# Order of tiles in the last attention, and smaller steps in a gated attention

## The reference

```python
def gla_mixer(h, w_in, w_gk2, b_gk, g_onorm, w_out):      # gated attention, 4 heads
    ...
    gk = gk_low @ w_gk2 + b_gk
    log_a = jax.nn.log_sigmoid(gk) / GLA_GATE_TAU
    b = jnp.cumsum(log_a, axis=3)                         # the gate sums, within chunks of 64
    q_e = q * jnp.exp(b); k_e = k * jnp.exp(-b)
    ...
    o = rms_norm(o, g_onorm).reshape(B, S, GLA_V)
    return (o * jax.nn.silu(gate)) @ w_out

def mla_mixer(h, positions, w_in, g_qa, w_qb, g_kva, w_kvb, w_out):   # last attention, 16 heads
    ...
    q = rms_norm(c_q, g_qa) @ w_qb                        # per head 128 plain + 64 rotary columns
    kv = rms_norm(c_kv, g_kva) @ w_kvb                    # per head 128 key + 128 value columns
    q = concatenate([q_nope, rope(q_rope)]); k = concatenate([k_nope, rope(k_rope)])
    p = softmax(causal(q @ k.T * scale))
    return (p @ v * silu(gate)) @ w_out
```

## Time and profile before

| | us |
|---|---|
| median of 3 runs | 2226.57 |
| lowest, highest | 2223.46, 2227.17 |
| the profiled execution | 2226.45 |
| its span | 2224.7 |
| TensorE busy in it | 2145.7 |
| VectorE busy | 1312.7 |
| ScalarE busy | 1158.4 |

### The profile page before, as it was taken

How to read it: one execution, slowest core, us unless ns; L and a number is a source line. 1 busy time by engine, 2 the same in 40 slices (tenths; PEclk the granted TensorE clock), 3 DMA queues, 4 the chain that set the end, 5 groups by cost and what they waited for, 6 DMA issues and landing times.

```text
span 2224.7 us, 46503 instructions
## 1 busy us (share of the span) xinstructions
PE 2145.7 (96%) x17596; PEld 2104.9 (95%) x17596; DVE 1312.7 (59%) x1641; ACT 1158.4 (52%) x1544; POOL 283.3 (13%) x325
## 2 busy tenths in 40 slices
PE   5999999999999999999999999999999979999996
PEld 5999999999999999999999999999998969899996
DVE  5655664544557666666765545655665465755644
ACT  5444545555546555555554444644554445656542
POOL 2000000010110111111111100001010123111112
PEclk8999999999999999999999999999999989999998
DMA  4454545555555555555545555445444434444453
GB/s 150 172 183 174 189 163 198 194 187 202 189 189 192 186 188 189 187 183 181 187 186 208 193 218 212 146 178 190 171 169 170 171 131 147 157 151 152 155 183 113
DMA packets 54927, 393.83 MB, mean 177 GB/s; under 512 B 6097, under 2 KB 6225, under 8 KB 7522
## 3 DMA queue, kind: packets, MB, share of 16 engines
q1 hardware_dynamic: 54432, 392.19, 49.2%
q10 hardware_dynamic: 450, 1.02, 0.1%
HBM read 391.09 MB, written 2.10 MB: 177 GB/s over the span
## 4 chain that ended last, share of the span: by engine, by line
PE 80%; issue 13%; POOL 3%; DVE 2%; ACT 2%; DMA 0%; POOLq 0%; DVEq 0%; ACTq 0%
PE acc L554 23%; PE acc L555 23%; PE acc L556 23%; PE tok L596 2%; PE tok L598 2%; PE tok L597 2%; POOL n_lo L1927 1%; POOL sumsq_g L1918 1%; PE att L614 1%; POOL x L1940 0%; POOL probs L2080 0%; DVE rstd L1345 0%; POOL probs L2077 0%; PE att L788 0%; PE att L864 0%
## 5 line engine op out<-in xcount | busy, mean ns | idle before, releaser
L1337 DVE TENSOR_TENSOR w_lo<-raw,w_hi 128x1024 fp32r<-128x1024 f32 x740 | 907.0, 1239 | 728.2 <-ACT w_hi L921 726.1
L921 ACT ACTIVATE w_hi<-raw 128x1024 fp32r<-128x1024 f32 x740 | 770.0, 1056 | 594.7 <-PE acc L556 363.5
L554 PE MATMUL acc<-n_hi,w_hi 128*128 128x256 f32 x3488 | 986.7, 283 | 26.8 <-POOL n_lo L1927 19.4
L555 PE MATMUL acc<-n_lo,w_hi 128*128 128x256 f32 x3488 | 979.6, 281 | 0.0
L556 PE MATMUL acc<-n_hi,w_lo 128*128 128x256 f32 x3488 | 979.4, 281 | 0.0
L554 PEld LDWEIGHTS acc<-n_hi,w_hi 128*128 128x128 f32 x3488 | 668.7, 192 | 30.1 <-issue 20.2
L555 PEld LDWEIGHTS acc<-n_lo,w_hi 128*128 128x128 f32 x3488 | 662.0, 190 | 0.5
L556 PEld LDWEIGHTS acc<-n_hi,w_lo 128*128 128x128 f32 x3488 | 660.8, 189 | 0.0
L555 PE MATMUL acc<-f_lo,w_hi 128*128 128x256 f32 x688 | 193.5, 281 | 0.0
L556 PE MATMUL acc<-f_hi,w_lo 128*128 128x256 f32 x688 | 193.5, 281 | 0.0
L554 PE MATMUL acc<-f_hi,w_hi 128*128 128x256 f32 x688 | 193.5, 281 | 0.0
(11 more groups left out here) (313 smaller groups left out, 2950.8 us busy)
## 6 DMA issues: line engine op xcount, KB each, us to landing
raw<-stream_in SPq DMA_DIRECT2D x370, 1024.0 KB, 4.8
x<-x_in SPq DMA_DIRECT2D x4, 512.0 KB, 7.4
out<-x SPq DMA_DIRECT2D x4, 512.0 KB, 2.6
v_bias<-v_bias_in ACTq DMA_DIRECT2D x1, 512.0 KB, 8.9
par<-params_in ACTq DMA_DIRECT2D x1, 287.0 KB, 5.5
pos_i<-positions_in ACTq DMA_DIRECT2D x1, 128.0 KB, 6.8
gk<-gk_in ACTq DMA_DIRECT2D x1, 68.0 KB
```

The source lines that it names most:

```text
L554: nc.tensor.matmul(out, w_hi[:, s, wc], hi[:, k, :], start=first, stop=False)
L555: nc.tensor.matmul(out, w_hi[:, s, wc], lo[:, k, :], start=False, stop=False)
L921: nc.scalar.activation(w_hi[:, s, :], raw[:, s, :], ACT.Copy).then_inc(hi_ready, 1)
L1337: nc.vector.tensor_tensor(w_lo[:, s, :], raw[:, s, :], w_hi[:, s, :].bitcast(fp32), ALU.subtract).then_inc(lo_ready, 1)
```

## The change

In the last attention the rotary queries come first: u0 rotary queries (acc0), u1 empty, u2 and u3 queries and keys of heads 0 and 1 (acc1, acc0), u4 and u5 those of heads 2 and 3 (acc1, acc0), u6 and u7 values. The layout in memory stays; SyncE loads the first three chunks of each pass in the order 2, 0, 1. The scores of heads 0 and 1 come before the values. The rotary block goes from j=5 to j=1 on VectorE, the copies of queries to j=2 and 4, of keys to j=3 and 5, the first logits from j=7 to j=6, the first exponentials from j=8 to j=6. In the gated attention the gate sums of heads 1 to 3 go from j=2 to j=8, 10 and 12. The end of each head works tile by tile: three products at j=22, the fourth at j=23, four copies to `og_hi` of one tile each, low parts of tiles 2 and 3 singly; the split of j=23 goes behind them on both engines.

```diff
@@ sync
+            mla_at = base["mla"][0][0] // 2
+            mla_end = mla_at + 2 * A_HEADS
+            with sp.Fori(1, mla_at // 2) as i:
                 for c in range(2):
+                    load(2 * i + c, c, 2 * i + c)
+            with sp.Fori(0, A_HEADS // 4) as i:
+                for c, source in enumerate((2, 0, 1, 3, 4, 5, 6, 7)):
+                    load(8 * i + (mla_at + c), c % 2, 8 * i + (mla_at + source))
...
@@ tensor, last attention
+                last = pair_tile(i, 0, 0, 0, 0)
+                unit("mla", i, 1)
+                last.then_inc(unit_done, 2)
                 for n in range(2):
-                    pair_tile(i, 2 * n, 0, n, 0).then_inc(unit_done, 1)
-                    pair_tile(i, 2 * n + 1, 1, n, A_TILES).then_inc(unit_done, 1)
-
-                last = pair_tile(i, 4, 0, 2, 0)
-                unit("mla", i, 5)
-                last.then_inc(unit_done, 2)
-                token_tiles("mla", i, 6, 2, 2, 4 * A_V, c_hi, c_lo, k0=A_TILES)
-                taken(pe, 0, "mla", i, 2)
-                taken(pe, 1, "mla", i, 1)
+                    pair_tile(i, 2 * n + 2, 1, n, 0).then_inc(unit_done, 1)
+                    pair_tile(i, 2 * n + 3, 0, n + 1, A_TILES).then_inc(unit_done, 1)
+                taken(pe, 1, "mla", i, 0)
+                taken(pe, 0, "mla", i, 1)
 
                 pe.wait_ge(krm_ready, 4)
                 scores(i, 0)
                 scores(i, 1)
+                token_tiles("mla", i, 6, 2, 2, 4 * A_V, c_hi, c_lo, k0=A_TILES)
...
@@ scalar, gated attention
-                    split("gla", i, j)
+                    if j != 23:
+                        split("gla", i, j)
...
+                    if j in (22, 23):
+                        for n in (range(3) if j == 22 else range(3, 4)):
+                            act.wait_ge(og_ready, FREE + 4 * i + (n + 1))
+                            nc.scalar.activation(og_hi[:, 4 * i + n, :], o_norm[:, n, :], ACT.Copy)\
+                                .then_inc(oghi_ready, 1)
                     if j == 23:
...
+                        split("gla", i, j)
...
@@ vector, gated attention
+                def product(n):
+
+                    dve.wait_ge(osg_ready, 4 * i + (n + 1))
+                    nc.vector.tensor_tensor(o_norm[:, n, :], o_norm[:, n, :], o_sg[:, n, :],
+                                            ALU.mult).then_inc(og_ready, 1)
...
                         if n == 3:
-                            split("gla", i, j)
+                            low(2)
+                            product(3)
+                            low(3).then_inc(oglo_ready_dve, 1)
...
-                    if first and j == 2:
-                        for hd in range(1, G_HEADS):
-                            gate_sums(hd)
+                    if first and j in (8, 10, 12):
+                        gate_sums(j // 2 - 3)
...
@@ vector, last attention
-                    if j in (1, 3):
-                        n = j // 2
+                    if j in (3, 5):
+                        n = j // 2 - 1
                         unit_is_done("mla", i, j)
-                        nc.vector.tensor_copy(kn[:, 2 * n:2 * n + 2, :], acc[1][:, :])\
-                            .then_inc(acc_taken[1], 1)
-                    if j == 5:
-                        taken(dve, 0, "mla", i, 2)
+                        nc.vector.tensor_copy(kn[:, 2 * n:2 * n + 2, :], acc[0][:, :])\
+                            .then_inc(acc_taken[0], 1)
+                    if j == 1:
+                        taken(dve, 0, "mla", i, 0)
...
-                    if j in (7, 12):
+                    if j in (6, 12):
```

More of the change, by code:

```diff
@@ L519, in _, with load @@
                     .then_inc(raw_ready[c], 16)
-            with sp.Fori(1, N_CHUNKS // 2) as i:
-                for c in range(2):
[L523 to L526, removed]
+            def load(n, slot, source):
+                sp.wait_ge(lo_ready, 2 * n - 2)
+                sp.dma_start(raw[:, 2 * slot:2 * slot + 2, :],
+                             stream_in[source].rearrange("p (u n) -> p u n", u=2)).then_inc(raw_ready[slot], 16)
+            mla_at = base["mla"][0][0] // 2
+            mla_end = mla_at + 2 * A_HEADS
+            with sp.Fori(1, mla_at // 2) as i:
+                for c in range(2):
+                    load(2 * i + c, c, 2 * i + c)
+            with sp.Fori(0, A_HEADS // 4) as i:
+                for c, source in enumerate((2, 0, 1, 3, 4, 5, 6, 7)):
+                    load(8 * i + (mla_at + c), c % 2, 8 * i + (mla_at + source))
+            with sp.Fori(mla_end // 2, N_CHUNKS // 2) as i:
+                for c in range(2):
+                    load(2 * i + c, c, 2 * i + c)
             for g in range(KT // 4):
@@ L1291, in _ @@
                             nc.scalar.activation(va[:, t, :], tok[t][:, :], ACT.Copy).then_inc(tok_taken, 1)
-                    if j in (8, 12):
-                        for n in range((j - 8) // 2, (j - 8) // 2 + 2):
+                    if j in (6, 12):
+                        for n in range((j - 6) // 3, (j - 6) // 3 + 2):
                             act.wait_ge(neg_ready, 4 * i + n + 1)
@@ L1632, in gla, with low @@
                 first = isinstance(i, int)
+                def product(n):
+                    dve.wait_ge(osg_ready, 4 * i + (n + 1))
+                    nc.vector.tensor_tensor(o_norm[:, n, :], o_norm[:, n, :], o_sg[:, n, :],
+                                            ALU.mult).then_inc(og_ready, 1)
+                def low(n):
+                    dve.wait_ge(oghi_ready, 4 * i + (n + 1))
+                    return nc.vector.tensor_tensor(og_lo[:, 4 * i + n, :], o_norm[:, n, :],
+                                                   og_hi[:, 4 * i + n, :].bitcast(fp32), ALU.subtract)
                 for j in range(24):
@@ L1722, in gla @@
                                 in1=o_rstd[:, :], op0=ALU.mult, op1=ALU.mult))
-                    if j == 23:
                         chain.wait()
-                        dve.wait_ge(osg_ready, 4 * i + 4)
-                        nc.vector.tensor_tensor(o_norm[:, :, :], o_norm[:, :, :], o_sg[:, :, :],
-                                                ALU.mult).then_inc(og_ready, 1)
-                        dve.wait_ge(oghi_ready, 2 * i + 2)
-                        nc.vector.tensor_tensor(og_lo[:, bass.ds(4 * i + 2, 2), :], o_norm[:, 2:4, :],
-                                                og_hi[:, bass.ds(4 * i + 2, 2), :].bitcast(fp32),
-                                                ALU.subtract).then_inc(oglo_ready_dve, 1)
-                    else:
-                        split("gla", i, j)
+                        for n in range(3):
+                            product(n)
+                    split("gla", i, j)
                     if first and j == 3:
```

24 lines of the change are left out of this document (11 added, 13 removed).

## The result

The changed kernel takes 2230.97 us (median of 11 runs, 2229.46 to 2232.71). The kernel before, run beside it, takes 2227.17 us (11 runs, 2223.46 to 2228.59). The ratio is 1.0019, with a 95% interval from 1.001 to 1.0028: 3.8 us more, 0.17%. The prediction was 2227.0 us, no change that can be told. The profiled execution took 2230.97 us, its span is 2228.8 us.

A forecast was written before the change was run, and what follows sets the result against it. TensorE's work plus the stretches in which it stands bound the kernel. Attention +7.0, first gated head -5.1 and last head's output -1.3 made +0.6 us on 2226.45: 2227.0 us, range 2218 to 2232.

The forecast's parts named there:

- Waits removed from the attention: Last attention: waits for q_rope, probs and kn go, 12.8 us, and one clock fall of 1.5 us behind them.
- The walk to kn(0): Last attention, VectorE's order ahead of the kn(0) copy: TensorE stands 3.47 us before u5 in passes two to four.
- ScalarE's start of the pass keeps its times: Second attention pass, starting at 1951.00: q_r takes qn's place at 1954.67, w_lo(u4) starts at 1956.25.
- First pass: Last attention's first pass: u5 at 1913.4 instead of 1907.0, 6.4 us of new idle time, 0.8 already at u2.
- The clock in the attention: Last attention: three clock falls after the change against one before, 1.5 us each, +3.0 us net (-1.5 to +4.5).
- Rival 2: Last attention: the clock holds, with no or one fall, 2222.5 to 2224.0 us; 20 in 100.
- One sign of being wrong: Last attention: a later pass more than 1 us off 54 plus its fall would show the prediction wrong.
- First gated head: First gated head: q_sb no longer held by gate sums, -3.5 us, and the fall behind, -1.6; part -5.1 us.
- Last head's output: Last gated head's end: low(3) ends earlier and TensorE goes on at about 1719.85, -1.3 us (-2 to -0.5).
- rival 3: Gated attention's head boundaries: w_lo(u27) late, up to 1.5 us paid in each of three heads, 2231.5 us; 12 in 100.
- rival 4: Gated attention: its parts give nothing since another wait takes their place, 2233 us; 4 in 100.
- Rival 1: Last attention: the rotary block is covered and u5 doesn't wait, 2205.8 us; 10 in 100.

The follow-up runs named there:

- the three experiments that keep the old attention: Kernel before with the gated attention's part alone (2219.28 us), with the gate sums moved alone (2221.23 us), with the tile-by-tile head end alone (2223.36 us).
- exchanged waits: Changed kernel with ScalarE's two waits ahead of the copy of q_r exchanged, q_rope's first, then unit u0's: 2225.9 us.
- the half-block kernel: Changed kernel with four of the eight rotated pieces moved behind the copy of kn(0): 2222.68 us.
- the gate sums alone: Kernel before with only the gate sums of heads 1 to 3 moved to j=8, 10 and 12: 2221.23 us.
- the gated parts alone: Kernel before with only the gated attention's part of the change, the last attention as before: 2219.28 us, ratio 0.9965.
- the halves: Kernel before with only the last attention's part of the change, 2236.34 us, and with only the gated attention's part, 2219.28 us.

## Why the prediction was right, and where its terms were off

The time came out inside the range, 3.97 us over the forecast and 1 us under the range's upper edge. The change is a little slower: the interval of the ratio is 2.2 to 6.2 us, and the forecast's +0.6 lies outside it, though +3.8 is less than the 4.5 us that the prediction called telling. So the mechanism came out, and one of its terms was too small. The repeated profiles of the two kernels close the sum. Up to the start of the first head's values the ten profiles with the new gate sums take 1443.1 to 1445.2 us, mean 1443.8, the four without 1448.8 to 1449.8, mean 1449.3: -5.5. The last head's output gives -1.2, the attention +10.6 (in the second profiles of both +10.7). That is +3.9, and the medians differ by 3.8. How close this is owes something to chance: in the three experiments that keep the old attention it had two falls and took 220.7 to 221.0 us, not 218.6, while the last projection took 3.4 us less (below).

- **Waits removed from the attention: right.** All nine are gone, and the reordered loads cost nothing: no wait for w_lo but the one at u2. From before's 218.6 us to the 204.8 us without a wait for kn are -13.8; the steps have -14.3 for it (12.8, the fall's 1.5) and 0.8 back at u2.
- **The walk to kn(0): right but for one step.** From w_lo(u4) to w_lo(u5) 6.12 us (forecast 6.11), two splits 2.28 (2.28), kn to TensorE 0.81 (0.81). The step that failed is "ScalarE's start of the pass keeps its times": q_r started 4.48 us behind the pass's start, not 3.67, since the copy now has two waits and the table load stands behind the first. The exchanged waits show that this is the cause and give 0.77 of a microsecond per pass. Against it, TensorE itself was 0.4 us later at u5 than the forecast, because its 96 matmuls ran at 117.8 ns where the second pass of the earlier trace rows had 113.3. So the wait was 3.87 instead of 3.47 us in passes two to four, +1.2 us.
- **First pass: right by two errors.** The wait was forecast 5.6 us at u5 and 0.8 at u2; it was 5.57 and 0.86. The copy came 0.55 us later than forecast, TensorE too. The copy's delay is the rotary block beside GpSimd's product (below).
- **The clock in the attention: mis-sized.** Forecast three falls at 1.5 us. All four waits had one, and two were of double length: 7.2 to 7.6 us instead of 4.5, +2.7 to +3.1. This is the largest miss. The term had one size for every fall, worked out from the single falls of the earlier trace rows. Rival 2, that the clock holds, is refuted. The Trainium skill's rule (TensorE: Matmul & The Clock Gate, "HAM oscillation — how this bites in real kernels"), a fall in every such wait, told there of waits for loads between short bursts of matmuls, was nearer to it; the traces agree for the changed kernel's waits for kn of 3.7 us and more. Shorter waits went either way: those of 1.9 us in the half-block kernel all had a fall, one of 2.9 us with the exchanged waits had none, and of the waits for probs of 1.2 to 2.4 us one in four had a fall in the two profiles of the kernel before and two in four in the three experiments that keep the old attention.
- **One sign of being wrong came up.** The prediction had named a later pass more than 1 us off 54 plus its fall. At 1.5 us a fall the second pass (57.34 us) is 1.8 over; with the 2.6 us that its fall really took it is 0.7 over. It points at the same term.
- **First gated head: right.** w_lo(u6) at 1436.88 and q_sb at 1438.02 are 0.38 and 0.37 us from the forecast, which the whole stage is late by in this profile. That the wait is gone here is in part luck: TensorE came late itself, and where it didn't, 1.4 us were left (the gate sums alone). Forecast -5.1, over all profiles -5.5. In this profile alone it gave -3.6, since the clock fell for twice as long under the gate logits, in a stretch ahead of the edit.
- **Last head's output: right.** From the head's end to TensorE 6.25 us (forecast 6.15), og_lo 1.9 us (forecast 1.8), -1.2 (forecast -1.3).
- **No charge at the head boundaries: right.** 264.86 us in both profiles; rival 3 is refuted, and rival 4 by the gated parts alone, which win 8.0 us.
- **Rival 1**, the covered block, had the right price: 2205.8 us forecast, 2207.0 measured once the copy stood ahead of the block. The change lacked this one step of order.

The forecast +0.6 us, +1.2 for the waits, +2.7 for the clock, -0.3 for the removed waits and -0.3 in the gated parts make +3.9.

Left open: the halves sum to +1.1 us, the whole is +3.8; the intervals of the halves are 3 us wide each way, which is enough to hold this, and the two paces are in them. What sets the length of a fall, and why 8 of the 20 waits for probs had one and 12 had none, was not tried.

## What to carry to other kernels

When a tile is moved to the front of a shared accumulator bank, list what the draining engine has in its own order ahead of the next copy out of that bank. Here 4.5 us of rotary block (1956.74 to 1961.20), for which nothing waited when it came later, stood with a split ahead of the 0.7 us copy that TensorE needed, and exchanging them was worth 24 us. A wait that is removed also removes the slow clock behind it, while halving the waits gave back the half and kept all four falls: here the last bit of a wait was worth more than the first. And before a difference of 3 us in an untouched stage is explained, profile the same kernel twice.

## What the runs showed of the hardware

- **Two paces at one clock.** In long stretches without a wait, at granted clock 1.00, the same float32 matmuls of 256 columns stand 113.3 or 117.8 ns apart, and the pace stays for a stage of 80 to 90 us. The gated output projection of the kernel before had one in one profile and the other in the next (83.4 and 80.3 us). The last projection took 92.0 us in both profiles of either kernel and 88.6 in the three experiments that keep the old attention. Nothing in the profile that was read tells what sets it.
- **A table load stands behind the first of two waits.** An activation with two waits had its ACT_TABLE_LOAD of 1.28 us between them: behind TensorE's tile in one order, ahead of it in the other. With TensorE's tile as the only wait, in the kernel before, it ran ahead of it too (the copy of qn started 3.67 us into its pass). Whether the chip does this or the program as it was built isn't shown. The order of two waits, which looks indifferent in the code, moved the load by 0.8 us.
- **Falls of two lengths.** Clock falls behind the four waits of 3.7 to 5.4 us cost 1.4 and 1.6 us, or 2.1 and 2.6. After three waits of 1.9 us for the same tile they came as well. Other waits had them at times: the one of 1.9 us for og_lo in seven of nine profiles, the one of 3.1 us in three of four, those for probs (1.2 to 2.4 us) in 8 of 20. Matmuls on ones with an unused result kept the clock at 1.00 in all four passes.
- **VectorE and GpSimd block each other.** In the first pass of the changed kernel both engines' rotary products fall together:

```profile
1897.71 1.23 DVE L1351 TENSOR_TENSOR w_lo<-raw,w_hi 128x1024 fp32r<-128x1024 f32 x1 [0.22 <-DVE kr_m L1844]
1898.86 0.96 DVE L1872 TENSOR_TENSOR rope_t<-q_r,cosine 128x256 f32<-128x256 f32 x1
1899.74 0.96 DVE L1874 TENSOR_TENSOR rope_t<-q_r,sine 128x256 f32<-128x256 f32 x1
...
1897.83 1.71 POOL L2090 TENSOR_TENSOR rope_t<-q_r,cosine 128x256 f32<-128x256 f32 x1 [5.68 <-DVE kr_m L1844]
```

  VectorE's products take 0.96 us instead of 0.41, GpSimd's first one 1.71 instead of 0.76, and the way from w_lo(u4) to w_lo(u5) is 6.70 us here (1897.71 to 1904.41) and 6.12 in the other passes. The prediction's estimate by the exclusive lock of the Trainium skill (SBUF — State Buffer, "SBUF: two separate sides") was 0.75 us for this pass, against none by the rows; it came to 0.58.
